# Adding expert rows per token tile on TensorE, in PSUM, in a two-layer mixture-of-experts step

## The chip, the cores and the metric

The kernel runs on one core of one Trainium2 chip. The metric is the device time of one execution, in microseconds (us). Lower is better.

## The reference, cut to what matters

A step of a two-layer transformer over 384 tokens (128 of context, 256 latent), model width 1024, everything in float32. Each layer mixes tokens (three kinds of attention and an output projection), and then applies a mixture of experts, which is what the change touches:

```python
def hier_moe(h, router_group, router_expert, w_gate, w_up, w_down):   # 4 groups of 8 experts, FF = 256
    g_sel = argmax(ht @ router_group)                  # one group per token
    top_v, top_i = lax.top_k(e_in, 2)                  # two experts inside it
    top_w = softmax(top_v) * g_w                       # their two weights
    y = sum over the two experts e of  top_w_e * (silu(ht @ w_gate[e]) * (ht @ w_up[e])) @ w_down[e]
x = layer_norm(ALPHA * x + gate * y, ln2_w, ln2_b)     # ALPHA = 4 ** 0.25, ends the layer
```

Each of the 384 tokens sends one row to each of two of 32 experts. Each expert has 3 MB of weights (three matrices of 1 MB), so a layer reads 96 MB of expert weights.

## The kernel before, in words

The five engines have one instruction stream each and meet through semaphores. `x` holds the tokens in three tiles of 128 (tile 0 context). A layer is: a front (projections, attention, output projection, first layer norm, router), the expert loop, possibly an item loop, and the end (weighting, second layer norm).

**Experts.** The 32 experts are worked in 16 pairs. A pair has 128 slots, 64 for each expert (`SLOTS`). From the ranks of tokens inside their experts, VectorE builds one-hot marks and TensorE turns them into indices (`select`, `places_of`, `indices`). GpSimd fetches the 128 token rows of a pair by an indirect DMA from `token_rows` in HBM (`fetch`, L2225), TensorE turns them (`rows_T`, L1215) and multiplies (`hidden`, L1243: the two experts stand in the two column halves of the array, products with 64 stationary columns; `down`, L1267). ScalarE and VectorE copy one half each of the 128 result rows of width 1024 (`rows_half`, L1555 and L2046) into one of two buffers `yb`, and GpSimd writes them by an indirect DMA to `expert_rows` in HBM (`scatter`, L2231), at row 1 + 2 * token + choice.

**Items.** Rows of rank 64 and above of an expert don't fit. `most` and `overflow` on VectorE find the pairs that have such rows, and write a list. An item (`item` on each engine) is one pair and one further round of 64 slots per expert. Its marks and indices are made ahead, for the first item in the expert loop at pairs 10 and 11 (`ITEM_STEP`), its six weight blocks are loaded by SyncE (`load_item`, L844), its matmuls are L1215, L1276, L1324, L1332 and L1344, and its rows go to `expert_rows` by L2247. The loop count is read from memory on every engine.

**End of a layer.** When all scatters have landed, ScalarE issues three reads (L1640), one per tile: each token's two rows, 1 MB. VectorE then takes, tile by tile, first row times first weight (L2172), plus second row times second weight (L2173), times `gate2` (L2174), plus ALPHA * x (L2176), moments (L1854, L1860, L1861), and the normalisation (`normalise`, L1869, then L1871 with a power that GpSimd makes, L2218). `ln2_done` counts the tiles; TensorE turns a tile for the next layer's front (L957) when its count has come, and goes on with the projections (L969, L962).

**Order of loads.** SyncE issues all weight loads in program order, each 1 MB into one of 17 places (12 in `ring`); each waits for the unit that lay there. `places_of_loads` works the places out ahead. In the last 12 freed ring places of a layer come the item's weights, `ln2` and `gate2`, and the first loads of the next layer. Expert weights are prefetched as far as places come free.

Of the kernel before, what the change touches and what calls it, by code (L numbers as in the profile page):

```python
# [21 lines left out]
U32 = mybir.dt.uint32  # L22
ALU = mybir.AluOpType
# [3 lines left out]
P = 128  # L27
# [32 lines left out]
ROUNDS_MAX = TOKENS // SLOTS  # L60
# [4 lines left out]
OVER_CODES = (ROUNDS_MAX - 1) * PAIRS  # L65
# [51 lines left out]
GATH = (7168, 9216, 3072)  # L117
# [4 lines left out]
K_COS = K_IOTA + SLOTS  # L122
# [11 lines left out]
K_MHALF = K_THR + ROUNDS_MAX  # L134
K_TOK = K_MHALF + 3
K_CODE = K_TOK + TILES
K_16 = K_CODE + OVER_CODES
K_COLS = K_16 + ROUNDS_MAX - 2


def shape_constants():
# [8 lines left out]
    k[:, K_IOTA:K_IOTA + SLOTS] = np.arange(SLOTS)  # L150
# [24 lines left out]
    k[:, K_THR:K_THR + ROUNDS_MAX] = SLOTS * np.arange(ROUNDS_MAX)  # L175
# [4 lines left out]
    k[:, K_16:K_16 + ROUNDS_MAX - 2] = PAIRS * np.arange(1, ROUNDS_MAX - 1)  # L180
# [121 lines left out]
LATE = ("ln2", "gate2")  # L302
# [35 lines left out]
def places_of_loads():  # L338


    spots, items, late, last_in, count = {}, [], [], [], [0] * PLACES
    free = deque((p, None) for p in range(RING))
    for l in range(DEPTH):
# [10 lines left out]
        items.append(left[:PAIR_UNITS])  # L354
        late.append(dict(zip(LATE, left[PAIR_UNITS:])))
        last_in.append({spots[l, u][0]: (l, u) for u in gone})
        free = deque(left[PAIR_UNITS + len(LATE):] + [(p, (l, ("item", m))) for m, (p, _) in enumerate(items[l])]
                     + [(late[l][n][0], (l, ("late", n))) for n in LATE])
    return spots, items, late, last_in


SPOT, ITEM_SPOT, LATE_SPOT, LAST_IN = places_of_loads()


# [3 lines left out]
ITEM_STEP = PAIRS - 5  # L368

# [35 lines left out]
def build(nc, x_prompt, x_sample, c, cache_na_k, cache_na_v, state_ret, cache_diff_k, cache_diff_v, c_ctx,  # L405
# [12 lines left out]
    with ExitStack() as ctx:  # L418
# [94 lines left out]
        osel = at(GSEL, TILES, 2, SLOTS)  # L513
# [4 lines left out]
        gath = [at(i, 2, D) for i in GATH]  # L518
# [8 lines left out]
        tab = route(TILES, PAIRS, 4)  # L527
        idxf = route(PAIRS * 2)
        idxu = route(PAIRS * 2).bitcast(U32)
        oidxf = route(2)  # L530
        oidxu = route(2).bitcast(U32)
        orow = route(1).bitcast(U32)
# [10 lines left out]
        pmax = route(PAIRS)  # L543
# [4 lines left out]
        steps = route(ITEMS_MAX, ROUNDS_MAX - 2)  # L548
        shift = route(ITEMS_MAX)
        n_items = route(1)  # L550
        iotar = route(SLOTS)
# [17 lines left out]
        rows_out = [signal(f"rows_out{i}", 16 * PAIRS // 2) for i in range(2)]  # L569
# [58 lines left out]
        o_full = [signal(f"o_full{s}", 16) for s in range(PAIR_UNITS)]  # L628
# [8 lines left out]
        o_out, o_stored = signal("o_out", 16), signal("o_stored", 1, start=1)  # L637
# [26 lines left out]
        def item_pair(eng, l, rel):  # L664

            return eng.value_load(items[0:1, bass.ds(l * ITEMS_MAX + rel, 1)], min_val=0, max_val=PAIRS - 1)
# [9 lines left out]
        def wait_released(eng, l, unit):  # L676
# [22 lines left out]
            elif kind == "late":  # L699
                eng.wait_ge(ln2_done.sem, ln2_done.at(l, TILES))  # L700
            elif kind == "pair":
# [23 lines left out]
        def _(sp):  # L725
# [29 lines left out]
            def late_loads(l):  # L755

                for name in LATE:
                    wait_released(sp, *LATE_SPOT[l][name][1])
                    for k in range(2):
                        if name == "ln2":  # L760
                            sp.dma_start(late_tile(l, name, k), (ln2_w, ln2_b)[k][l:l + 1].to_broadcast([P, D]))\
                                .then_inc(ln2_in.sem, 16)
                        else:
                            sp.dma_start(late_tile(l, name, k), modd[l, 1, k:k + 1, D:2 * D].to_broadcast([P, D]))\
                                .then_inc(gate2_in.sem, 16)
# [69 lines left out]
            def load_item(l, o0, i):  # L835

                p = item_pair(sp, l, item_place(l, o0, i))
                for m in range(PAIR_UNITS):
                    kind, which = m // 2, m % 2
                    place, (_, (_, pair, part, _)) = ITEM_SPOT[l][m]  # L840
# [3 lines left out]
                    sp.dma_start(ring[:, place, :], expert_unit(l, 2 * p + which, kind)).then_inc(o_full[m].sem, 16)  # L844

            sp.wait_ge(cond_zero.sem, 3)
            for l in range(DEPTH):
# [6 lines left out]
                if l:  # L854
                    for t in range(TILES):
                        sp.wait_ge(gathered[t].sem, gathered[t].at(l - 1, 16))
# [26 lines left out]
                late_loads(l)  # L883
# [9 lines left out]
        def _(pe):  # L893
# [296 lines left out]
            def first_places(l, tiles):  # L1190

                for j in tiles:
                    pe.wait_ge(pair0_marked.sem, pair0_marked.at(l, j + 1))
                    mm = pe.matmul(ps[:, IDX_BANK[0], 0:4], gsel[:, j, 0:2, :].rearrange("p e s -> p (e s)"),
                                   tab[:, j, 0, :], start=(j == 0), stop=(j == TILES - 1))
# [3 lines left out]
            def places_of(l, k):  # L1199
# [5 lines left out]
                for i in range(a, b):  # L1205
                    e = 2 * (i % GPAIRS)
                    for j in range(TILES):
                        mm = pe.matmul(ps[:, IDX_BANK[k], 2 * e:2 * e + 4],  # L1208
                                       gsel[:, j, e:e + 2, :].rearrange("p e s -> p (e s)"),
                                       tab[:, j, i, :], start=(j == 0), stop=(j == TILES - 1))  # L1210
# [62 lines left out]
            def item_index(p):  # L1273

                for j in range(TILES):
                    mm = pe.matmul(ps[:, 7, 0:4], osel[:, j, :, :].rearrange("p e s -> p (e s)"),  # L1276
                                   tab[:, j, bass.ds(p, 1), :].rearrange("p o k -> p (o k)"),
                                   start=(j == 0), stop=(j == TILES - 1))
                mm.then_inc(o_idx.sem, 1)

            def experts(l):
# [6 lines left out]
                for i in range(PAIRS):  # L1288
# [10 lines left out]
                    if i == ITEM_STEP:  # L1299
                        first = items_before(pe, l)  # L1300
                        p = item_pair(pe, l, 0)
                        pe.wait_ge(o_sel.sem, o_sel.at(first + l, 1))
                        pe.wait_ge(xt_dve.sem, xt_dve.at(l, i + 2))
                        item_index(p)
                    hidden_T(l, i)

            def item(l, o0, i):

                pe.wait_ge(o_xr_in.sem, o_xr_in.at(i, 16 * (l + 1)))
# [4 lines left out]
                p = item_pair(pe, l, item_place(l, o0, i, 1))  # L1314
                pe.wait_ge(o_xt_dve.sem, o_xt_dve.at(i, 1))
                pe.wait_ge(o_sel.sem, o_sel.at(i + l, 2))
                item_index(p)
# [1035 lines left out]
```

## Time and profile before

| | |
|---|---|
| timed runs | 1209.1, 1213.51, 1214.12 us (median 1213.51) |
| profiled execution | span 1211.0 us (the page has no other time of it), 16524 instructions |
| PE (TensorE) busy | 1053.2 us, 87% |
| PE weight loads | 703.2 us, 58% |
| DVE (VectorE) | 432.5 us, 36% |
| ACT (ScalarE) | 209.3 us, 17% |
| POOL (GpSimd) | 181.7 us, 15% |
| DMA | 343.83 MB in 102993 packets, mean 284 GB/s |

The profile is of one execution. Engines overlap, so busy shares say little about what sets the end; that is read from the chain of waits, which is followed back from the last instruction. In 40 slices of the span TensorE and the DMA engines look like this (digits are tenths, GB/s is what the DMA engines moved):

```profile
PE   4899999989979999987739999999896999998840
...
PEclk9799999999879999989859999999995999999985
DMA  8997222685999999999869312238957899999961
```

Layer 0 ends in slices 20 and 21 (from 577 to 623 us), layer 1 in the last two. The long stretches of 9 in the DMA line are the expert loops.

### The profile page before, as it was taken

How to read it: one execution, taken by the hardware profiler on the slowest of the kernel's cores; microseconds unless marked ns; L12 is line 12 of the kernel's file. 1: busy time of each engine (PE TensorE's matmuls, PEld its weight loads, DVE VectorE, ACT ScalarE, POOL GpSimd, SP SyncE). 2: the span in 40 equal slices, each digit the busy share in tenths (PEclk: the TensorE clock that was granted, in tenths of full speed). 3: DMA queues.
4: the chain of work that ended last, by engine and by line, in shares of the span. 5: the costliest groups of instructions: out<-in, count | busy, mean ns of one | idle time of the engine just before them, and what ended most of it. 6: DMA issues, size and time to landing. Idle time of an engine off the chain costs nothing.

```text
span 1211.0 us, 16524 instructions
## 1 busy us (share of the span) xinstructions
PE 1053.2 (87%) x6588; PEld 703.2 (58%) x6589; DVE 432.5 (36%) x1016; ACT 209.3 (17%) x524; POOL 181.7 (15%) x176
## 2 busy tenths in 40 slices
PE   4899999989979999987739999999896999998840
PEld 1766878568655555554328577775785655554510
DVE  0044544257741212100164344543676212111117
ACT  0322334100111111101113222421001111111000
POOL 0440020051111111101113000202301111111001
PEclk9799999999879999989859999999995999999985
DMA  8997222685999999999869312238957899999961
GB/s 345 251 276 230 70 83 71 229 293 236 352 420 417 419 419 418 418 420 419 317 225 319 99 64 77 83 110 314 332 182 286 349 418 419 418 419 419 410 247 63
DMA packets 102993, 343.83 MB, mean 284 GB/s; under 512 B 20530, under 2 KB 61538, under 8 KB 70404
## 3 DMA queue, kind: packets, MB, share of 16 engines
q1 hardware_dynamic: 88832, 316.58, 68.6%
q0 software_dynamic: 12352, 16.74, 4.5%
q10 hardware_dynamic: 1732, 9.45, 2.0%
q8 instruction: 54, 0.88, 0.3%
q14 instruction: 23, 0.19, 0.0%
HBM read 341.92 MB, written 26.16 MB: 304 GB/s over the span
## 4 chain that ended last, share of the span: by engine, by line
PE 63%; SPq 13%; DMA 11%; DVE 4%; issue 4%; POOL 3%; ACT 2%; POOLq 0%; DVEq 0%; ACTq 0%
PE ps L969 16%; SPq L828 13%; PE ps L1243 11%; PE ps L962 8%; PE ps L1146 7%; PE ps L1267 5%; DMA arena<-in_exp_w_gate 2%; DMA ring<-in_exp_w_down 2%; DMA arena<-in_exp_w_down 2%; PE ps L1215 2%; DMA ring<-in_w_mod 2%; PE ps L911 1%; PE ps L1062 1%; PE ps L1208 1%; PE ps L1108 1%
## 5 line engine op out<-in xcount | busy, mean ns | idle before, releaser
L1243 PE MATMUL ps<-ring,arena 128*64 128x256 f32 x1488 | 208.7, 402 | 14.4 <-DMA ring<-in_exp_w_up 6.8
L969 PE MATMUL ps<-ring,arena 128*128 128x256 f32 (+1 forms) x960 | 200.8, 367 | 5.8 <-ACT arena L1477 5.8
L969 PEld LDWEIGHTS ps<-ring,arena 128*128 128x128 f32 x960 | 170.9, 195 | 28.9 <-issue 8.6
L1243 PEld LDWEIGHTS ps<-ring,arena 128*64 128x64 f32 x1488 | 128.4, 144 | 70.1 <-issue 27.7
L1267 PE MATMUL ps<-ring,arena 128*64 128x512 f32 x360 | 96.6, 608 | 10.0 <-DMA ring<-in_exp_w_down 7.5
L2039 DVE TENSOR_TENSOR arena<-arena,ps 128x256 f32<-128x256 f32 x32 | 13.5, 421 | 253.8 <-PE ps L1243 143.3
L962 PE MATMUL ps<-arena,ring 128*128 128x384 f32 x288 | 96.9, 490 | 0.7 <-ACT arena L1482 0.5
L1146 PE MATMUL ps<-ring,arena 128*128 128x256 f32 x384 | 90.0, 398 | 0.0
L1146 PEld LDWEIGHTS ps<-ring,arena 128*128 128x128 f32 x384 | 76.8, 202 | 11.4
L2225 POOL DMA_INDIRECT arena<-token_rows,arena x32 | 33.4, 1045 | 279.1 <-PE ps L1215 154.0
L962 PEld LDWEIGHTS ps<-arena,ring 128*128 128x128 f32 x288 | 53.3, 190 | 36.8 <-issue 1.8
L1555 ACT ACTIVATE arena<-ps 128x512 f32<-128x512 f32 x32 | 19.1, 597 | 255.3 <-PE ps L1267 255.3
L2046 DVE COPY arena<-ps 128x512 f32<-128x512 f32 x32 | 22.1, 692 | 108.5 <-PE ps L1267 108.5
L1267 PEld LDWEIGHTS ps<-ring,arena 128*64 128x64 f32 x360 | 28.8, 138 | 51.2 <-issue 48.7
L2231 POOL DMA_INDIRECT expert_rows<-arena x32 | 33.0, 1031 | 159.2 <-DVE arena L2046 157.3
L1215 PE MATMUL ps<-kc,arena 128*128 128x128 f32 x264 | 48.6, 308 | 7.3 <-DMA arena<-token_rows,arena 4.3
L911 PE MATMUL ps<-ring,cond 128*32 128x512 f32 x360 | 48.9, 653 | 6.6 <-DMA ring<-in_w_mod 6.6
L1215 PEld LDWEIGHTS ps<-kc,arena 128*128 128x128 f32 x264 | 35.2, 196 | 32.4 <-issue 25.0
L1243 PE MATMUL ps<-arena 128*64 128x256 f32 x320 | 49.4, 395 | 3.1 <-DMA arena<-in_exp_w_up 2.3
L1482 ACT ACTIVATE arena<-ps 128x256 f32<-128x256 f32 (+2 forms) x60 | 24.6, 415 | 152.2 <-PE ps L969 104.1
L2218 POOL TENSOR_TENSOR ln_s<-ln_s,kc 128x1 f32<-128x1 f32 x12 | 18.3, 1526 | 145.7 <-DVE ln_s L1861 145.7
L1243 PEld LDWEIGHTS ps<-arena 128*64 128x64 f32 x320 | 30.0, 141 | 13.3 <-issue 3.5
(264 smaller groups left out, 1279.1 us busy)
## 6 DMA issues: line engine op xcount, KB each, us to landing
ring<-in_exp_w_gate SPq DMA_DIRECT2D x49, 1024.0 KB, 21.3
ring<-in_exp_w_up SPq DMA_DIRECT2D x48, 1024.0 KB, 21.7
ring<-in_exp_w_down SPq DMA_DIRECT2D x47, 1024.0 KB, 28.5
ring<-in_w_mod SPq DMA_DIRECT2D x45, 1024.0 KB, 5.5
ring<-in_w_in SPq DMA_DIRECT2D x24, 1024.0 KB, 13.2
arena<-in_exp_w_down SPq DMA_DIRECT2D x12, 1024.0 KB, 20.1
arena<-in_exp_w_up SPq DMA_DIRECT2D x11, 1024.0 KB, 24.2
arena<-in_exp_w_gate SPq DMA_DIRECT2D x9, 1024.0 KB, 29.1
```

Of the source, the lines that this page charges most:

```text
L828: sp.dma_start(dst, src).then_inc(ring_full[place].sem, 16)
L911: mm = pe.matmul(ps[32 * g:32 * g + 32, bank, 0:512], cond[:, ch, :], weights[:, 512 * g:512 * g + 512], start=(ch == 0), stop=(ch == CH - 1))
L962: mm = pe.matmul(out[:, 0:TOKENS], w[:, ch, :], hT[:, ch, :], start=(ch == 0), stop=(ch == CH - 1))
L969: mm = pe.matmul(out[:, 0:w], hT[:, ch, where * P:(where + 1) * P], unit(l, name)[:, ch, 0:w], start=(ch == 0), stop=(ch == CH - 1))
L1146: mm = pe.matmul(ps[:, 2 * t + u // 2, (u % 2) * UCOL:(u % 2 + 1) * UCOL], mixed(ch, t), unit(l, name)[:, ch, :], start=(ch == 0), stop=(c ...
L1215: mm = pe.transpose(ps[:, 7, k * P:(k + 1) * P], src[:, 4 * b + k::CH], ident)
L1243: mm = pe.matmul(ps[64 * w:64 * w + 64, 2 * (i % 2) + kind, 0:FF], xgT[i % 2][:, ch, w * SLOTS:(w + 1) * SLOTS], weights[:, ch * FF:(ch + ...
L1267: mm = pe.matmul(ps[64 * w:64 * w + 64, 5 + n, :], hidT[i % 2][:, j, 64 * w:64 * w + 64], weights[:, j * D + n * 512:j * D + (n + 1) * 512 ...
L1482: act.activation(dst, job_view(j, n, dst), ACT.Copy, scale=RET_SCALE if kind == "rkT" else 1.0)\
L2046: dve.tensor_copy(yb[i % 2][:, 512:D], ps[:, 6, :]).then_inc(row_dve.sem, 1)
L2225: pool.indirect_dma_start(xr[i % 2], None, h2d, bass.IndirectOffsetOnAxis(ap=idxu[:, 2 * i + 1:2 * i + 2], axis=0), bounds_check=TOKENS, o ...
L2231: pool.indirect_dma_start(rows, bass.IndirectOffsetOnAxis(ap=idxu[:, 2 * i:2 * i + 1], axis=0), yb[i % 2], None, bounds_check=ROWS - 1, oo ...
```

## The change

1. **The last pair's rows** (pair 15) are no longer scattered (`SCATTERED = 15`). VectorE makes, for this pair, a matrix of marks times gate weights (`marks_of_last`, after `gate_weights`, at pair 11), TensorE turns it into `ptl` (at pair 12) and at the end multiplies it with `yb[1]`, per tile.
2. **Items** are one expert with 128 slots. Their marks times gate weight are turned into `pti[t]`; their rows stay in `yi`. Before an item overwrites them, the rows of the item before are flushed: six products into PSUM, and VectorE adds them times gate2 / ALPHA to x. The first item flushes zeros. An item loads three weight blocks and stores nothing.
3. **Weighting.** The two gathered rows of a token are multiplied by diagonal matrices of the two weights (zero for rows that were never scattered) in the same PSUM banks (`final_sums`). VectorE multiplies by gate2 from PSUM (`combine`) and goes on as before, in the order combine 0, 1, normalise 0, combine 2, normalise 1, 2.
4. **Reading back** is issued by SyncE into ring places, after `gate2` has been loaded ahead of the items, and before the next layer's first loads; tile 2's after `ln2`.
5. `expert_rows` is set to zero once, in layer 0, by eight DMAs of GpSimd from the `decay` tile.

```diff
+ITEM_SLOTS = 2 * SLOTS
+SCATTERED = PAIRS - 1
+FINAL_BANKS = ((4, 7), (0, 1), (2, 3))
+FLUSH_BANKS = ((2, 3), (5, 6), (4, 2))
...
 # SyncE, end of a layer
+                load_gate2(l)
                 wait_alone(sp, items_known, items_known.at(l, 1))
...
-                late_loads(l)
+                for k in range(2):
+                    wait_alone(sp, rows_out[k], rows_out[k].at(l, rows_out[k].step))
+                load_rows_back(l, 0)
+                load_rows_back(l, 1)
+                load_ln2(l)
+                load_rows_back(l, 2)
...
 # TensorE
+            def turn_marks(outs):
+                for j in range(TILES):
+                    mm = pe.transpose(outs[j], gw[:, j, :], ident)
+                return mm
...
+            def final_sums(l, o1):
+                pe.wait_ge(row_act.sem, row_act.at(l, PAIRS))
+                pe.wait_ge(row_dve.sem, row_dve.at(l, PAIRS))
+                pe.wait_ge(pt_copied.sem, pt_copied.at(l, 1))
+                pe.wait_ge(pi_zeroed.sem, pi_zeroed.at(l, 1))
...
+                for t in range(TILES):
+                    outs = [ps[:, FINAL_BANKS[t][n], :] for n in range(2)]
+                    halves_ = [slice(512 * n, 512 * n + 512) for n in range(2)]
+                    for n in range(2):
+                        pe.matmul(outs[n], ptl[:, t, :], yb[(PAIRS - 1) % 2][:, halves_[n]], start=True, stop=False)
+                    for n in range(2):
+                        pe.matmul(outs[n], pti[t], yi[:, halves_[n]], start=False, stop=False)
+                    pe.wait_ge(gathered[t].sem, gathered[t].at(l, 16))
+                    for k in range(2):
+                        for n in range(2):
+                            mm = pe.matmul(outs[n], diag(k, t), gath(l, t)[:, k, halves_[n]], start=False, stop=(k == 1))
+                    mm.then_inc(final_ready.sem, 1)
...
+            def flush_half(t, n):
+                return pe.matmul(ps[:, FLUSH_BANKS[t][n], :], pti[t], yi[:, 512 * n:512 * n + 512], start=True, stop=True)
             def item(l, o0, i):
...
+                pe.wait_ge(pi_zeroed.sem, pi_zeroed.at(l, 1))
+                pe.wait_ge(row_act.sem, row_act.at(l, PAIRS))
+                pe.wait_ge(row_dve.sem, row_dve.at(l, PAIRS))
+                for t in range(TILES - 1):
+                    for n in range(2):
+                        mm = flush_half(t, n)
+                    mm.then_inc(o_flush.sem, 1)
+                flush_half(TILES - 1, 0)
                 pe.wait_ge(o_xr_in.sem, o_xr_in.at(i, 16 * (l + 1)))
...
                 for kind, done in ((0, o_gate), (1, o_up)):
...
                     for ch in range(CH):
-                        for w in range(2):
-                            mm = pe.matmul(ps[64 * w:64 * w + 64, kind, 0:FF],
-                                           xgT[0][:, ch, w * SLOTS:(w + 1) * SLOTS],
...
+                        mm = pe.matmul(ps[:, kind, 0:FF], xgT[0][:, ch, :],
+                                       ring[:, ITEM_SPOT[l][kind][0], ch * FF:(ch + 1) * FF],
...
+                    if kind == 0:
+                        pe.wait_ge(o_flushed.sem, o_flushed.at(i, 1))
+                        flush_half(TILES - 1, 1).then_inc(o_flush.sem, 1)
+                pe.wait_ge(o_gw.sem, o_gw.at(i, 1))
+                turn_marks([ps[:, 3, t * P:(t + 1) * P] for t in range(TILES)]).then_inc(o_pt.sem, 1)
...
 # ScalarE, in an item
+                act.wait_ge(o_pt.sem, o_pt.at(i, 1))
+                for t in range(TILES):
+                    ins = act.activation(pti[t], ps[:, 3, t * P:(t + 1) * P], ACT.Copy)
+                ins.then_inc(o_pi.sem, 1)
...
 # VectorE, in an item
+                for t in range(TILES):
+                    dve.wait_ge(o_flush.sem, o_flush.at(i, t + 1))
...
+                    for n in range(2):
+                        ins = dve.scalar_tensor_tensor(zt[:, half], ps[:, FLUSH_BANKS[t][n], :], 1.0 / ALPHA, gate2[:, half], ALU.mult, ALU.mult)
...
+                    dve.tensor_tensor(x[:, t, :], x[:, t, :], zt, ALU.add).then_inc(o_flushed.sem, 1)
...
 # VectorE, after the expert loop
+                for t in range(TILES):
+                    for k in range(2):
+                        ins = dve.tensor_scalar(diag(k, t), ident, wtsm[:, k, t:t + 1], None, ALU.mult)
+                ins.then_inc(diag_ready.sem, 1)
...
                 rows_half(l, PAIRS - 1)
+                dve.wait_ge(rows_out[0].sem, rows_out[0].at(l, rows_out[0].step))
+                dve.wait_ge(hidT_ready.sem, hidT_ready.at(l, PAIRS))
+                for t in range(TILES):
+                    ins = dve.memset(pti[t], 0.0)
+                ins.then_inc(pi_zeroed.sem, 1)
+                dve.wait_ge(gate2_in.sem, gate2_in.at(l, gate2_in.step))
...
+                combine(l, 0, chain)
+                combine(l, 1, chain)
+                normalise(l, 0, chain)
+                combine(l, 2, chain)
+                normalise(l, 1, chain)
+                normalise(l, 2, chain)
...
 # GpSimd
+                if l == 0:
+                    for n in range(ZERO_STEPS):
+                        pool.dma_start(rows[1 + n * 96:1 + (n + 1) * 96]..., zeros).then_inc(rows_zeroed.sem, 16)
...
-                    scatter(l, i)
+                    if i < SCATTERED:
+                        scatter(l, i)
```

`rows_out[0]` counts the scatters of the even pairs; its last one is now pair 14's. `yb[0]`, from which that scatter reads, is a scratch tile of the flush.

## Rows read from the trace of the kernel before

**Rows 1.** The page: the span, and the chain that ended last, by engine.

```profile
span 1211.0 us, 16524 instructions
...
PE 63%; SPq 13%; DMA 11%; DVE 4%; issue 4%; POOL 3%; ACT 2%; POOLq 0%; DVEq 0%; ACTq 0%
```

**Rows 2.** The chain of waits, 640 to 1160 us: start, duration (us), what.

```profile
649.29 13.83 PE ps L969 x64
...
1041.73 3.63 PE ps L1243 x32
...
1129.38 28.47 DMA ring<-in_exp_w_down
```

**Rows 3.** SyncE's waits, 700 to 840 us: total us, times, longest.

```profile
SPq L828 <- PE ps L969: 95.1, 7, 19.2
```

**Rows 4.** Timeline, end of layer 0: start, us, engine, line, operation [idle before].

```profile
577.91 0.97 POOL L2231 DMA_INDIRECT expert_rows<-arena  x1 [14.57 <-DVE arena L2046]
...
581.23 0.71 PE L1215 MATMUL ps<-kc,arena 128*128 128x128 f32 x4
...
581.34 0.69 DVE L2046 COPY arena<-ps 128x512 f32<-128x512 f32 x1 [4.28 <-PE ps L1267]
...
585.69 1.44 PE L1276 MATMUL ps<-arena 128*128 x6 [2.35 <-DVE arena L2055]
...
587.06 9.55 PE L1324 MATMUL ps<-ring,arena 128*64 128x256 f32 x64
...
598.18 3.65 PE L1344 MATMUL ps<-ring,arena 128*64 128x512 f32 x16 [0.47 <-ACT arena L1564]
...
601.88 0.69 DVE L2085 COPY arena<-ps 128x512 f32<-128x512 f32 x1 [4.74 <-PE ps L1344]
...
613.36 0.75 DVE L2172 TENSOR_SCALAR arena<-arena 128x1024 f32<-128x1024 f32 x1 [10.78 <-DMA arena<-expert_rows]
...
621.55 1.28 DVE L1871 SCALAR_TENSOR_TENSOR x<-x,ln_s,ring 128x1024 f32<-128x1024 f32 x1 [0.53 <-POOL ln_s L2218]
...
622.98 1.94 PE L957 MATMUL ps<-kc,x 128*128 128x128 f32 x8 [21.14 <-DVE x L1871]
...
627.15 10.01 PE L969 MATMUL ps<-ring,arena 128*128 128x256 f32 x32 [2.23 <-ACT arena L1477]
```

**Rows 5.** Timeline, end of layer 1, same columns.

```profile
1168.01 0.69 DVE L2046 COPY arena<-ps 128x512 f32<-128x512 f32 x1 [3.94 <-PE ps L1267]
...
1177.37 0.75 DVE L2172 TENSOR_SCALAR arena<-arena 128x1024 f32<-128x1024 f32 x1 [8.66 <-DMA arena<-expert_rows]
...
1179.47 1.22 DVE L2174 TENSOR_TENSOR arena<-arena,ring 128x1024 f32<-128x1024 f32 x1
...
1183.74 1.28 DVE L1869 SCALAR_TENSOR_TENSOR x<-x,ln_s,ring 128x1024 f32<-128x1024 f32 x1
...
1204.26 1.28 DVE L1871 SCALAR_TENSOR_TENSOR x<-x,ln_s,ring 128x1024 f32<-128x1024 f32 x1 [0.51 <-POOL ln_s L2218]
```

**Rows 6.** Landing time of the scatter issued at 577.91 us (line 2231).

```profile
DMA to landing us min/median/max: 8.4/8.4/8.4
```

**Rows 7.** Landing time of the scatter issued at 1164.93 us (line 2231).

```profile
DMA to landing us min/median/max: 4.1/4.1/4.1
```

**Rows 8.** The chain of waits at the end of layer 1.

```profile
1172.57 4.77 DMA arena<-expert_rows
```

**Rows 9.** Windows: length, busy (x) PE/PEld/DVE/ACT/POOL, granted clock, DMA share, GB/s.

```profile
578.00:582.00 4.00, 3.94 (x20) 1.55 (x16) 0.66 (x1) 0.62 (x2) 0.88 (x1) 1.00 1.00 406
...
586.00:588.00 2.00, 2.00 (x12) 1.60 (x13) 0.74 (x4) 0.00 (x0) 0.00 (x0) 0.50 0.86 349
...
592.00:594.00 2.00, 2.00 (x22) 1.31 (x20) 0.00 (x0) 0.39 (x1) 0.00 (x0) 1.00 0.56 217
```

**Rows 10.** VectorE groups by line and shape: busy us, mean ns.

```profile
L1692 DVE TENSOR_SCALAR decay<-kc,lg 128x128 f32<-128x128 f32 x12 | 2.5, 280 | 0.0
...
L1733 DVE TENSOR_TENSOR arena<-arena,kdec 128x384 f32<-128x384 f32 x8 | 3.9, 554 | 10.5 <-PE ps L962 10.5
```

More of the change, by code:

```diff
@@ L338, in places_of_loads @@
 def places_of_loads():
-    spots, items, late, last_in, count = {}, [], [], [], [0] * PLACES
+    spots, items, late, gath, last_in, count = {}, [], [], [], [], [0] * PLACES
     free = deque((p, None) for p in range(RING))
@@ L568, in build @@
         xr_in = [signal(f"xr_in{i}", 16 * PAIRS // 2) for i in range(2)]
-        rows_out = [signal(f"rows_out{i}", 16 * PAIRS // 2) for i in range(2)]
+        rows_out = [signal(f"rows_out{i}", 16 * len(range(i, SCATTERED, 2))) for i in range(2)]
         y_out = signal("y_out")
@@ L835, in load_item @@
             def load_item(l, o0, i):
[L837 to L840, printed above, removed]
+                e = item_expert(sp, l, item_place(l, o0, i))
+                for kind in range(ITEM_UNITS):
+                    place, (_, (_, pair, part, _)) = ITEM_SPOT[l][kind]
                     last, before = (gate_ready, up_ready, down_ready)[part], (o_gate, o_up, o_down)[kind]
@@ L843, in load_item @@
                     sp.wait_ge(before.sem, before.at(i, 0))
-                    sp.dma_start(ring[:, place, :], expert_unit(l, 2 * p + which, kind)).then_inc(o_full[m].sem, 16)
+                    sp.dma_start(ring[:, place, :], expert_unit(l, e, kind)).then_inc(o_full[kind].sem, 16)
             sp.wait_ge(cond_zero.sem, 3)
@@ new lines, in combine @@
+            def combine(l, t, chain):
+                zt = gath(l, t)[:, 1, :]
+                b0, b1 = FINAL_BANKS[t]
+                dve.wait_ge(final_ready.sem, final_ready.at(l, t + 1))
+                dve.tensor_tensor(zt.rearrange("p (a b) -> p a b", a=2), ps[:, b0:b1 + 1:b1 - b0, :],
+                                  late_tile(l, "gate2", min(t, 1)).rearrange("p (a b) -> p a b", a=2), ALU.mult)                    .then_inc(combined.sem, 1)
+                dve.wait_ge(combined.sem, combined.at(l, t + 1))
+                chain.link(dve.scalar_tensor_tensor(x[:, t, :], x[:, t, :], ALPHA, zt, ALU.mult, ALU.add))
+                moments(t, chain, var2)
@@ L2065, in item_indices @@
-                ins.then_inc(o_link.sem, 1)
+                token = ps[:, 7, 0:1]
+                dve.tensor_scalar(oidxf, token, 0.5, kc[:, K_EMPTY:K_EMPTY + 1], ALU.is_lt, ALU.mult).then_inc(o_link.sem, 1)
                 dve.wait_ge(o_link.sem, o_link.at(nth * 2, 2))
-                for w in range(2):
-                    hp, src = halves(7, 0, 1, w)
-                    ins = dve.tensor_tensor(oidxu[hp, :], oidxf[hp, :], src, ALU.add)
-                ins.then_inc(o_known.sem, 1)
+                dve.tensor_tensor(oidxu, oidxf, token, ALU.add).then_inc(o_known.sem, 1)
@@ L2142, in _ @@
                 copy_rows_T(l, 0)
-                most(l, chain)
                 overflow(l, chain)
```

304 lines of the change are left out of this document (170 added, 134 removed).

## The prediction

> **What bounds the kernel now.** I read the chain of waits first. Of the 1211.0 us span TensorE holds 63%, SyncE's queue 13%, DMA 11% [rows 1]. In layer 1 the chain runs on TensorE's own projections until pair 7's products at 1041.7 us, then on the weight stream (SyncE's queue), whose last block was issued at 1129.4 and landed 28.5 us later [rows 2]: up to there the layer is set by TensorE, after it by the stream. While TensorE sets it, SyncE waits for it (95.1 us for line 969 alone, [rows 3]), so nothing in the front of layer 1 is ahead of TensorE, and a late start of layer 1 moves everything behind it one for one. The weight stream does not absorb it: its ring places are freed by that same TensorE.
>
> So the change is worth what it does in two stretches, the two layer ends, read from the timeline. Layer 0: the last pair's rows are copied out by 582.03; one overflow item runs from 581.23 to 602.57 (21.3 us); its store and the reading back take until 613.36; tile 0 is finished at 622.83, and only then does TensorE turn it for layer 1 (622.98) [rows 4]. Layer 1 has no item: rows copied out by 1168.70, first weighted row at 1177.37, last normalisation ending 1205.54, then 5.5 us to the end [rows 5].
>
> **The number of items** depends on the data. The reference's router gives, on the kernel's inputs, one expert with 65 tokens in layer 0 (number 28; its neighbour has 40) and none above 64 in layer 1. So both kernels run one item in layer 0. It fetches three weight blocks in place of six, but its matmuls start without a wait for them now (index product ends 587.13, line 1324 starts 587.06 [rows 4]): the 3 MB saved are worth nothing.
>
> **The price of the new products.** 64 instructions of line 969 are 32 products of a 128x128 block with 256 columns and take 13.83 us [rows 2], 0.43 us each. With 512 columns that is 0.86; I take 0.87. The expert matmuls work on two column halves side by side and cost the same per pair, so a half-empty item gains nothing by being one expert: gate and up are 16 products of 256 columns, 6.9 us. The final sums are, per tile, 2 (last pair) + 2 (item) + 4 (two gathered rows times diagonal weights) products of 512 columns: 8 x 0.87 = 7.0 us, for three tiles 20.9 us, where TensorE had nothing to do. VectorE loses two steps per tile: its first tile was at 1177.37 to 1179.47 before the gate2 product, 2.1 us. What is left is a combine of 4.3 us (1179.47 to 1183.74) and a normalisation of 2.6 (two of 1.28) [rows 5]: 6.9 per tile. So TensorE and VectorE now pace each other at 7 us a tile.
>
> **Layer 1's end.** The memsets of the item's marks wait for the scatter of pair 14, issued 1164.93, landed 4.1 us later [rows 7]: 1169.03. Three memsets of 128x128 have no row; below, nothing, above, 0.28 us each (a tensor_scalar of that shape [rows 10]); I take 0.6 in all. TensorE starts at 1169.7, does four products (3.5) to 1173.2. SyncE issues the first read-back behind the same landing, at 1169.2; it took 4.77 [rows 8]: 1174.0. Tile 0's sum is ready at 1174.0 + 3.5 = 1177.5, tile 1's at 1184.5, tile 2's at 1191.4. VectorE: combine tile 2 to 1195.7, normalise tile 1 to 1198.3, tile 2 to 1200.9, against 1205.54: -4.6. For a lowered clock (below) I give back 0.5: **-4.1 us**. Pair 15's scatter (landing 1172.4) is what this end no longer waits for.
>
> **Layer 0's end.** Here the same memsets cost more. Pair 14's scatter was issued at 577.91 and took 8.4 us [rows 4, 6], because the weight queue was full (406 GB/s in that window [rows 9]): 586.3, plus 0.1 and 0.6, 587.0. The item in TensorE waits for it; its first instruction was at 581.23 [rows 4], so 5.8 us of a new wait. Behind it on TensorE is all of the item. (The queue is shorter now by 3 MB of item weights and the late rows, but still holds some 4 MB, about 10 us at 406 GB/s; so I keep 8.4, with the 4.1 of [rows 7] as the other end.)
> - Flush: five products, 4.35 us, though nothing has been summed yet for a first item. TensorE will have idled 5.7 us. In this trace it idled from 583.3 to 585.7 and then ran at clock 0.50 until about 592 (1.2 instead of 2.4 GHz) [rows 4, 9]; about 5.4 us at half speed lose 2.7. So 594.1.
> - Turning rows and making marks: 581.23 to 585.69 before [rows 4], and on VectorE one more product of 128x384 (0.55 [rows 10]) and a register load, less the three small mark instructions joined in one: +0.2, 598.8. Index product 1.4: 600.2.
> - Gate and up 6.9, the sixth flush product 0.9, and the same clock loss as now: line 1324 took 9.55 for 2 x 3.63 at full clock [rows 2, 4], 2.3. 610.2. VectorE's three flushed tiles (two 128x512 products and an addition of 128x1024, 2.7 each) end at 609.5, beside it.
> - Mark transposes 0.6, transposes of the hidden rows 0.5, ScalarE's three mark copies ahead of its hidden copy (1.1 + 0.4), four down products 3.5, copy 0.7: 616.6, against 602.57.
> - Final sums: 623.6, 630.6, 637.5. The reading back is done long before. VectorE takes combine 0, combine 1 and only then normalises tile 0: 630.6 + 4.3 + 2.6 = 637.5, against 622.83: +14.7.
> - The front of layer 1 then starts with a TensorE that was just busy. Before, its first 32 instructions of line 969 took 10.0 us [rows 4] for 6.9 by [rows 2]; ScalarE's drain of the turned tile, nearly 3 us, lies between, so I count back 1.0 only: **+13.7 us**.
>
> **What is hidden.** The gate weights, marks and diagonals (some 20 small VectorE instructions a layer, 0.3 to 0.6 us each, about 7 us) and the last pair's transposes stand in the expert loop, where the weight stream sets the time; without that cover they would cost up to 7 us a layer. The eight zeroing DMAs (3.1 MB, 8 us at 406 GB/s) are issued on GpSimd near 93 us of layer 0, ahead of its diff normalisation, long before VectorE needs them; uncovered, +8. SyncE's read-backs stand before layer 1's first weight loads; these are then issued near 590, needed after 637. The small loads, now behind these, come earlier than now.
>
> One rule speaks against the change. VectorE's six diagonals (0.28 us each [rows 10]) now run from about 577.1 to 578.8, beside the scatter issued at 577.91 [rows 4]. The Trainium skill (SBUF — State Buffer, "SBUF: two separate sides") says that a DMA issued by GpSimd cannot write its descriptors while VectorE runs an operation that takes both of its port pairs. By it the scatter, and with it the memsets, would be up to 0.9 us later in each layer, and the sum about 1.8 higher; no run here shows that yet.
>
> **Sum.** +13.7 - 4.1 = +9.6: the profiled span of 1211.0 becomes 1220.6. The page gives no other time for that execution; the timed runs' median is 1213.5 (1209.1 to 1214.1), 2.5 above the span. So 1223.
>
> **Rivals.**
> - *The item starts without the wait and with a fast clock.* If the scatter of pair 14 lands in 4.1 us or sooner and TensorE keeps its clock through the flush, layer 0 loses 4.3 + 2.7 less: +6.7, total +2.6, 1216. For it: the queue is shorter. Against: the six scatters issued between 545 and 584 us took 8.2 to 8.6, and [rows 6] is one of them.
> - *Not slower: the loss of layer 0 is absorbed.* If the weight stream of layer 1, which sets the time from 1041.7 on, could start as early as before, only the front would be late and the end would keep its -4.1: 1209.4. It decides from the point where SyncE is not waiting for TensorE. Against: [rows 3]; I give it little. The same result would come if the sums' products overlapped more than those of line 969.
> - *The cold clock reaches the final sums.* If TensorE's 1.5 us idle in layer 1 and the 1 us in the item let it fall, each end loses another 2.7: +15, 1228.5.
> - *The change does not do what it says:* more items than one. Each further one would add about 27 us (587.0 to 616.6, less the cold clock's 2.7); the router's counts speak against it.
>
> **Chances.** Forecast 0.58; first rival 0.15; absorbed 0.10; cold clock 0.13; rest 0.04. A difference of 0.5% (6 us) is about what can be told here: faster is below 1207.4 and gets 0.08 (half of the absorbed case, whose 1209.4 carries a few us of its own, and most of the rest); same, up to 1219.6, gets 0.22 (the first rival, the other half of the second, the lowest of the forecast's own spread); slower 0.70. The range 1211 to 1231 leaves out half of the absorbed case and the far tail.
>
> **What would show it.** Right: a TensorE gap of about 5 us before the item; line 957 of layer 1 near 637; sums of 7 us a tile, VectorE waiting for them; last normalisation 4 us earlier after the last copy than now. Wrong: the item's first product before 584, sums under 5 us a tile, or a weight stream in layer 1 that ends less than 10 us later than before.

## The result, and the profile after

| | before | after |
|---|---|---|
| timed runs | 1210.51 us median of 10 (1208.83 to 1215.79) | 1216.86 us median of 10 (1213.75 to 1220.08) |
| profiled execution | span 1211.0 us | span 1218.2 us, its own time 1220.08 us |

The ratio is 1.0049 with a 95% interval of 1.0033 to 1.0064: the changed kernel is 6 us slower. The prediction's 1223 us stands on the three runs of before that were known then (median 1213.5); all ten have their median 3.0 us lower. A profile is one execution, and executions of one kernel differ by some us: that of the changed kernel is the slowest of its ten (3.2 us above their median). So differences of whole spans are rough, and the readings below go by stretches and by the timed runs. In the sections below, line numbers are those of the kernel that the row is from.

The page of the changed kernel: the span, TensorE's and VectorE's busy time, the chain by engine [rows 1].

```profile
span 1218.2 us, 16695 instructions
...
PE 1099.9 (90%) x6665; PEld 724.6 (59%) x6666; DVE 437.7 (36%) x1042; ACT 210.8 (17%) x531; POOL 181.6 (15%) x181
...
PE 64%; SPq 13%; DMA 10%; DVE 5%; issue 4%; ACT 2%; POOL 2%; DVEq 0%; POOLq 0%; ACTq 0%
```

TensorE is busy 46.7 us longer, VectorE 5.2 us. Where that meets the path to the end is seen in the timeline. First the end of layer 0 (start, us, engine, line, operation, idle before it and what ended that), which answers to [rows 4]:

```profile
577.85 0.97 POOL L2363 DMA_INDIRECT expert_rows<-arena  x1 [14.85 <-issue]
...
580.92 0.69 DVE L2127 COPY arena<-ps 128x512 f32<-128x512 f32 x1 [3.07 <-PE ps L1304]
586.11 0.45 DVE L2299 MEMSET arena<- 128x128 f32 x3 [4.50 <-DMA expert_rows<-arena]
...
586.77 7.00 PE L1385 MATMUL ps<-arena 128*128 128x512 f32 x10 [5.88 <-DVE arena L2299]
...
593.60 0.60 PE L1252 MATMUL ps<-kc,arena 128*128 128x128 f32 x4
...
598.63 1.43 PE L1313 MATMUL ps<-arena 128*128 x6 [3.03 <-DVE arena L2173]
...
616.09 0.69 DVE L2211 COPY arena<-ps 128x512 f32<-128x512 f32 x1 [4.93 <-PE ps L1433]
617.09 1.96 PE L1347 MATMUL ps<-arena 128*128 128x512 f32 x4 [1.04 <-ACT arena L1662]
...
624.23 1.23 DVE L2161 TENSOR_TENSOR ring<-ps,ring 128x1024 f32<-128x1024 f32 x1 [7.45 <-PE ps L1353]
...
631.10 1.23 DVE L2161 TENSOR_TENSOR ring<-ps,ring 128x1024 f32<-128x1024 f32 x1 [2.52 <-PE ps L1353]
...
636.67 1.28 DVE L1959 SCALAR_TENSOR_TENSOR x<-x,ln_s,ring 128x1024 f32<-128x1024 f32 x1
...
638.11 1.13 PE L994 MATMUL ps<-kc,x 128*128 128x128 f32 x8 [0.18 <-DVE x L1959]
...
641.88 8.83 PE L1006 MATMUL ps<-ring,arena 128*128 128x256 f32 x32 [2.64 <-ACT arena L1563]
```

The reader is to see three things. The memsets of the item's marks wait for a scatter that was issued at 577.85, and TensorE stands idle for 5.88 us behind them. Then come 7.00 us of flush (line 1385) before the item's first row is turned (line 1252, 593.60). And the three sums end at 637.93, when VectorE has just finished tile 0 (637.95): the two engines arrive together, so another order on VectorE alone could start layer 1 no more than 0.2 us earlier. From the last pair's copy (580.92) to the turning of tile 0 for layer 1 (line 994) it is 57.19 us, against 41.64 before (581.34 to 622.98).

The end of layer 1 answers to [rows 5]:

```profile
1182.09 0.69 DVE L2127 COPY arena<-ps 128x512 f32<-128x512 f32 x1 [2.76 <-PE ps L1304]
...
1184.06 1.95 PE L1347 MATMUL ps<-arena 128*128 128x512 f32 x4 [2.02 <-DVE arena L2299]
...
1187.57 3.67 PE L1353 MATMUL ps<-ring,arena 128*128 128x512 f32 x8
...
1191.28 1.23 DVE L2161 TENSOR_TENSOR ring<-ps,ring 128x1024 f32<-128x1024 f32 x1 [8.08 <-PE ps L1353]
...
1198.14 1.23 DVE L2161 TENSOR_TENSOR ring<-ps,ring 128x1024 f32<-128x1024 f32 x1 [2.51 <-PE ps L1353]
...
1213.11 1.28 DVE L1959 SCALAR_TENSOR_TENSOR x<-x,ln_s,ring 128x1024 f32<-128x1024 f32 x1
```

From the copy to the last normalisation it is 31.02 us, against 36.25: 5.2 us are gained. The sums come every 6.87 us, and VectorE waits for TensorE (2.5 us before the second). From there on it waits no more: the third sum is ready when VectorE is free for it (1205.0). The rest is in the last few us, where SyncE waits for the other engines once its stores have landed. SyncE's waits, of before and then of after:

```profile
SPq L418 <- PEq L418: 2.6, 1, 2.6
```

```profile
SPq L428 <- PEq L428: 1.0, 1, 1.0
```

From the end of the last normalisation to the end of the span it is 5.5 us before and 3.8 after; 1.6 of that 1.7 us is this wait for TensorE's queue.

So the account of the profile is: end of layer 0 +15.6, its last copy 0.4 earlier, the stretch from line 994 to layer 1's last copy -1.1 (543.98 against 545.03 us), end of layer 1 -5.2, tail -1.7; together +7.2, which is the difference of the spans. The 0.4 and the 1.1 us are small against what this middle stretch does from one execution to another (540.9 to 544.1 us in the nine kernels with the change).

### The profile page after: what moved, and what is told of

Its sections match the earlier page's. It is cut to its first block, busy times and chain, and to the rows that moved or that the text cites. A ratio compares the mean times of both kernels' runs of the same rounds, so it can differ in the third digit from the quotient of the medians.

```text
span 1218.2 us, 16695 instructions
## 1 busy us (share of the span) xinstructions
PE 1099.9 (90%) x6665; PEld 724.6 (59%) x6666; DVE 437.7 (36%) x1042; ACT 210.8 (17%) x531; POOL 181.6 (15%) x181
## 4 chain that ended last, share of the span: by engine, by line
PE 64%; SPq 13%; DMA 10%; DVE 5%; issue 4%; ACT 2%; POOL 2%; DVEq 0%; POOLq 0%; ACTq 0%
PE ps L1006 16%; SPq L863 13%; PE ps L1280 10%; PE ps L999 7%; PE ps L1183 7%; PE ps L1304 5%; DMA ring<-in_exp_w_down 2%; DMA ring<-in_exp_w_gate 2%; DMA arena<-in_exp_w_down 2%; PE ps L1252 2%; DMA ring<-in_w_mod 2%; PE ps L948 1%; PE ps L1099 1%; PE ps L1245 1%; PE ps L1353 1%
## 5 line engine op out<-in xcount | busy, mean ns | idle before, releaser
L1280 PE MATMUL ps<-ring,arena 128*64 128x256 f32 x1488 | 205.1, 398 | 15.2 <-DMA ring<-in_exp_w_up 7.4
L1304 PE MATMUL ps<-ring,arena 128*64 128x512 f32 x360 | 96.5, 607 | 12.8 <-DMA ring<-in_exp_w_down 10.4
L1614 ACT ACTIVATE arena<-ps 128x384 f32<-128x384 f32 (+3 forms) x42 | 22.1, 527 | 89.0 <-PE ps L1119 60.8
## 6 DMA issues: line engine op xcount, KB each, us to landing
ring<-in_w_in SPq DMA_DIRECT2D x24, 1024.0 KB, 12.8
```

Source lines behind the costliest of these rows:

```text
L1280: mm = pe.matmul(ps[64 * w:64 * w + 64, 2 * (i % 2) + kind, 0:FF], xgT[i % 2][:, ch, w * SLOTS:(w + 1) * SLOTS], weights[:, ch * FF:(ch + ...
L1304: mm = pe.matmul(ps[64 * w:64 * w + 64, 5 + n, :], hidT[i % 2][:, j, 64 * w:64 * w + 64], weights[:, j * D + n * 512:j * D + (n + 1) * 512 ...
L1614: act.activation(dst, src, ACT.Copy).then_inc(probsT_copied.sem, 1)
```

## The experiments

Each kernel is timed beside the kernel before on its own chip. The table goes by the profile, with the two stretches just read, "layer 0" (start of the last copy to the turning of tile 0) and "layer 1" (start of the last copy to the start of the last normalisation step), in us:

| kernel | layer 0 | layer 1 | span | timed median, ratio to before (95%) |
|---|---|---|---|---|
| before | 41.64 | 36.25 | 1211.0 | 1210.51 |
| after | 57.19 | 31.02 | 1218.2 | 1216.86, 1.0049 (1.0033 to 1.0064) |
| e1_late_wait | 49.81 | 31.11 | 1209.6 | 1209.04, 0.9992 (0.9974 to 1.0009) |
| e2_no_flush | 49.44 | 31.00 | 1209.3 | 1210.67, 1.0002 (0.9985 to 1.0019) |
| e3_no_flush_no_wait | 42.38 | 30.99 | 1204.3 | 1202.28, 0.9933 (0.991 to 0.9956) |
| e6_flush_if_needed | 43.15 | 31.10 | 1203.6 | 1205.4, 0.9955 (0.9935 to 0.9975) |
| e8_products_if_needed | 43.51 | 29.34 | 1203.0 | 1203.41, 0.9938 (0.9919 to 0.9957) |
| e4_before_no_items | 23.95 | 36.27 | 1194.1 | 1192.63, 0.9838 (0.9811 to 0.9865) |
| e5_after_no_items | 23.75 | 31.04 | 1181.3 | 1185.45, 0.9795 (0.9761 to 0.983) |
| e7_no_item_products | 53.30 | 29.15 | 1211.1 | 1214.25, 1.0021 (1.0003 to 1.0039) |
| e9_last_pair_scattered | 53.39 | 35.89 | 1218.2 | 1220.74, 1.008 (1.0052 to 1.0109) |

### The wait for the scatter (e1)

VectorE waits for the scatter only ahead of the flush of x (and once more ahead of the combines), no longer ahead of the memsets that TensorE waits for.

```diff
-                dve.wait_ge(rows_out[0].sem, rows_out[0].at(l, rows_out[0].step))
                 dve.wait_ge(hidT_ready.sem, hidT_ready.at(l, PAIRS))
                 ...
+                dve.wait_ge(rows_out[0].sem, rows_out[0].at(l, rows_out[0].step))
                 zt = yb[0]
```

> The changed kernel, but VectorE waits for pair 14's scatter only where it first needs the buffer (before the flush of the item), no longer ahead of the memsets that TensorE's item waits for. Theory (the new wait of 5 us stands on the path and also cools TensorE's clock): TensorE's gap before the item goes from 5.9 to about 1.5 us, the flush takes 4.3 us in place of 7.0, the whole is 7 us faster than the changed kernel (about 1211, no difference from before). Rival (the item is paced by VectorE's chain, and TensorE would wait for it later): less than 2 us faster, about 1216.

Measured: 1209.04 us, ratio 0.9992, as the theory of the wait had it; layer 0 is shorter by 7.4 us. The timeline of e1 at the item's start:

```profile
581.58 0.45 DVE L2299 MEMSET arena<- 128x128 f32 x3
...
582.23 4.53 PE L1385 MATMUL ps<-arena 128*128 128x512 f32 x10 [1.36 <-DVE arena L2299]
...
586.60 0.60 PE L1252 MATMUL ps<-kc,arena 128*128 128x128 f32 x4
```

The idle time falls from 5.88 to 1.36 us, and the same five products take 4.53 instead of 7.00 us. The clock in windows shows why (length, busy time of PE/PEld/DVE/ACT/POOL, granted clock, DMA share, GB/s), first of after, then of e1:

```profile
587.00:590.00 3.00, 3.00 (x4) 1.25 (x5) 0.00 (x0) 0.00 (x0) 0.00 (x0) 0.50 0.89 314
590.00:592.00 2.00, 2.00 (x4) 0.79 (x3) 0.00 (x0) 0.00 (x0) 0.00 (x0) 0.57 1.00 406
592.00:594.00 2.00, 2.00 (x9) 1.04 (x7) 0.00 (x0) 0.00 (x0) 0.00 (x0) 1.00 0.99 408
```

```profile
582.00:584.00 2.00, 1.77 (x4) 0.87 (x5) 0.03 (x1) 0.00 (x0) 0.00 (x0) 1.00 0.41 170
584.00:586.00 2.00, 2.00 (x6) 0.95 (x5) 0.00 (x0) 0.00 (x0) 0.00 (x0) 1.00 0.30 125
```

After the long gap TensorE runs at 1.2 GHz, after the short one at 2.4. So the wait costs 4.5 us of idle time and 2.5 us of clock, 7.0 of the 7.4.

### The flush (e2, e3)

e2 takes the six flush products and VectorE's part of them out; e3 also lets the item start without the wait, which then stands only where `yi` and `pti` are written. With one item in layer 0 and none in layer 1, the flush adds zeros.

```diff
-                for t in range(TILES - 1):
-                    for n in range(2):
-                        mm = flush_half(t, n)
-                    mm.then_inc(o_flush.sem, 1)
-                flush_half(TILES - 1, 0)
...
-                    if kind == 0:
-                        pe.wait_ge(o_flushed.sem, o_flushed.at(i, 1))
-                        flush_half(TILES - 1, 1).then_inc(o_flush.sem, 1)
```

> The changed kernel without the flush of the item's rows (six products on TensorE, nine instructions on VectorE), which adds nothing where a layer has one item; the wait for pair 14's scatter stays where it is. Theory (the flush is on the path in full): 7.0 us for the first five products, 1 for the sixth, less about 0.5 for transposes that now run at the low clock: 7.5 us faster than the changed kernel, about 1210. Rival (flush hidden beside the rows' turning and VectorE's marks): under 2 us.

> Both: no flush, and the item on TensorE starts as soon as its rows are there, as in the kernel before. Theory: 5.4 us of wait, 7.0 and 1.0 of flush, 13.4 us faster than the changed kernel, about 1203.5, that is 0.5 to 0.6% faster than before. Rival (the front of layer 1 or the weight stream absorbs part): half of that, about 1210.

Measured: e2 1210.67 us, 1.0002, and e3 1202.28 us, 0.9933. Set against the changed kernel by the ratios that is 5.7 us less (expected 7.5) and 14.0 less (expected 13.4); layer 0 is 7.75 us shorter without the flush, 14.8 without both. In e2 the gap stays, and the transposes behind it pay the clock in place of the flush (1.09 us, where e3 takes 0.71):

```profile
586.19 1.09 PE L1252 MATMUL ps<-kc,arena 128*128 128x128 f32 x4 [6.39 <-DVE arena L2276]
```

```profile
581.51 0.71 PE L1252 MATMUL ps<-kc,arena 128*128 128x128 f32 x4
```

So the two costs add (wait 7.1 to 7.4, flush 7.4 to 7.75, together 14.8), and without them the end of layer 0 is within 0.7 us of before (42.38 against 41.64): from the item's rows to the turning of tile 0 the new sums take 21.8 us in e3, storing and reading back the item's rows and the weighting took 21.1 before.

### Both kernels without items (e4, e5)

```diff
-                chain.link(dve.tensor_scalar(later, found, 0.5, None, ALU.is_gt))
+                chain.link(dve.tensor_scalar(later, found, 1.0e9, None, ALU.is_gt))
```

e4 is the kernel before with this line and the eight zeroing DMAs, e5 the one after with this line.

> The kernel before with the item loop never entered (it leaves out the one row of rank 64 of layer 0) and with the eight zeroing DMAs of the change. It also shows what the zeroing costs. Theory (zeroing hidden): the item took 581.3 to 603.4; without it pair 15's scatter lands near 591 and the reading back ends near 596 in place of 613.4: 17 us faster than before, about 1193.5. Rival (the zeroing is on the path): 8 us less of a gain, about 1201.

> The changed kernel with the item loop never entered (the same row is left out). Theory (the change gains at a layer end without an item and loses by its item): the sums start near 587 in place of 617, 29 us faster than the changed kernel, about 1188, and about 5 us (2 to 7) faster than the kernel before without items. Rival (the weighting on TensorE is what makes the change slow, whatever the item does): slower than the kernel before without items, by 5 us or more.

Measured: 1192.63 against 1185.45 us. The ends of layer 0 are alike (23.95 and 23.75), the end of layer 1 is 5.2 us shorter, and the wait of the tail goes from 3.1 to 0.9 us; these two make 7.4 us, the medians differ by 7.2. The spans differ by 12.8 us; the 5.4 us more lie ahead of and between the ends. The profile of e4 is the slowest of its four runs (3.3 us above their median), that of e5 the fastest (2.3 below), which is as much, so they are left as spread between executions. Two things follow. Without items the change makes the kernel 7 us faster by the medians, 5 by the ratios (four runs each; the intervals of the ratios just overlap). And e4 came out as expected with the zeroing in it, so the 8 us of the zeroing are hidden. One trace of it is left: pair 14's scatter in layer 0 is issued 1.87 us after the start of its copy in e4, 1.86 in after and 1.54 in before, 0.3 us later with the zeroing; why is not shown.

### The item's products in the sums (e7), the last pair's rows (e9)

```diff
-                    for n in range(2):
-                        pe.matmul(outs[n], pti[t], yi[:, halves_[n]], start=False, stop=False)
```

> The changed kernel without the two item products of each tile's sum (it leaves out the item's rows; in layer 1 they add zeros). Six products a tile take 5.2 us, VectorE 6.9. Theory (TensorE sets the pace of both ends): layer 0's tile 0 is finished 4.3 us earlier (1.7 for the first sum, 2.6 because VectorE no longer waits for the second), layer 1 ends 2.4 us earlier, together 6.7 faster, about 1210. Rival (VectorE sets the pace already): under 1.5 us.

Measured: layer 0 3.9 us shorter, layer 1 1.9, together 5.8 for the 6.7 expected; timed 1214.25, by the ratios only 3.4 us better than after, half of what was expected, and this is not explained. (The spans differ by 7.1, but after's profile is its slowest run and this one lies 1.3 us under its median.) Four of the removed products stood ahead of the second sum, behind which VectorE finishes tile 0 (3.4 us), which is the price in layer 0. In layer 1 only the second tile's two products came off (1.7 us). The first sum now waits for the data, and from the second sum on VectorE sets the pace, so the third tile's are worth nothing:

```profile
1182.19 3.70 PE L1351 MATMUL ps<-ring,arena 128*128 128x512 f32 x8 [1.47 <-DMA ring<-expert_rows]
```

e9 scatters pair 15 again and drops the `ptl` products; the rest of the change stays.

```diff
-SCATTERED = PAIRS - 1
+SCATTERED = PAIRS
...
-                        pe.matmul(outs[n], ptl[:, t, :], yb[(PAIRS - 1) % 2][:, halves_[n]], start=True, stop=False)
```

> The changed kernel with the last pair scattered and read back as all others, so that six products a tile are left (item and gathered rows). Theory: layer 0 gains 4.3 us (as by leaving out the item's products; the later scatter has time to land), layer 1's reading back waits for pair 15's scatter, 4 us later, and gains 2.4 by the shorter sums: together 2.9 faster than the changed kernel, about 1213.5. Rival (keeping the last pair off HBM is what speeds up the end): slower by 4 us or more.

This expectation failed, and the rival's price was nearly met: timed 1220.74 us, by the ratios 3.8 us slower than after. (The spans are equal because this profile is its fastest run and after's its slowest.) Layer 0 is 3.8 us shorter, but layer 1 is 4.9 longer; that makes only 1.1 of the 3.8 us, the rest is not accounted for. Its timeline and its clock at the end of layer 1:

```profile
1178.62 0.97 POOL L2360 DMA_INDIRECT expert_rows<-arena  x1 [3.64 <-DVE arena L2125]
...
1182.56 0.80 SPq L798 DMA_DIRECT2D ring<-expert_rows  x2
...
1187.40 5.50 PE L1351 MATMUL ps<-ring,arena 128*128 128x512 f32 x8 [6.30 <-DMA ring<-expert_rows]
```

```profile
1184.00:1187.00 3.00, 0.00 (x0) 0.00 (x0) 0.00 (x0) 0.00 (x0) 0.00 (x0) 0.54 0.98 388
```

The read-back waits for one more scatter, TensorE idles 6.30 us, its clock falls to 0.54, and the first four products on the gathered rows take 5.50 us instead of 3.67. So keeping the last pair's rows out of the round trip is what earns the 5 us at the end of layer 1; it costs 3.8 us in layer 0, where the item hides that round trip.

### A version that beats both (e6, e8)

In e6 the flush runs only from a layer's second item on, behind branches on TensorE and VectorE, and TensorE's and VectorE's waits stand where e3 has them. Nothing is left out.

```diff
+                with pe.If(i > o0):
                     pe.wait_ge(pi_zeroed.sem, pi_zeroed.at(l, 1))
                     ...
                     flush_half(TILES - 1, 0)
+                with pe.If(i <= o0):
+                    pe.sem_inc(o_flush.sem, TILES)
```

> A complete version: as e3, but the flush stands in a branch that is taken from a layer's second item on. Theory: e3 plus a few branches on TensorE and VectorE, some 0.5 to 1.5 us: about 1204.5, 0.4 to 0.5% faster than before. Rival: a branch inside the loop costs more than 5 us on TensorE, and the gain over before is gone.

Measured: 1205.4 us, 0.9955, as expected. Layer 0 takes 43.15 us, 0.8 more than e3, which is the most that the branches can have cost there; 0.3 of it lies in the gate and up products (9.21 against 8.93 us). The timed medians lie 3.1 us apart, with intervals that overlap, so the whole price is not settled.

e8 adds `with pe.If(o1 > o0):` around the item's products in the sums.

> This is the version with the flush only from a layer's second item on (1205.4 us, ratio 0.9955, span 1203.6), and with the six products of the item's rows in the final sums issued only where the layer has an item at all. Theory: layer 0 has one item, so nothing changes there beyond three branches of TensorE; layer 1 has none and drops six products, 2.6 us of TensorE in all. Where these products were left out of both layers, layer 1's first sum then waited for the read-back of the scattered rows, so at most 1.8 us come off (the second and third tile), and the branches take some back: 1203.5 us, ratio 0.994. Rival: a branch on TensorE's queue inside each tile costs about 1 us (it can't run ahead of it), six of them in the two layers, and the version is slower than the one it is made from: 1207 us or more, ratio 0.998.

Measured: 1203.41 us, 0.9938, which is the theory's number. Layer 1 is 1.76 us shorter than in e6 and layer 0 0.4 longer, all of it in the gate and up products (9.57 against 9.21 us), ahead of the new branches; the rival's 1 us per branch is refuted. The 1.76 us are the second tile's products alone, as in e7, not the second and third tile's as expected. The timed gain of e8 over e6 (2.0 us, intervals that overlap) isn't settled by itself; the gain of either over before is.

## Why the prediction was right or wrong

**Layer 0's end: right, step by step.** Forecast for a last copy at 581.34; the measured starts are 0.42 us earlier for that reason alone.

| step | forecast | measured |
|---|---|---|
| item may start | 587.0 | 586.77 |
| flush done | 594.1 | 593.60 |
| marks ready | 598.8 | 598.63 |
| gate and up | 600.2 | 599.92 |
| item copied out | 616.6 | 616.78 |
| tile 0 finished | 637.5 | 637.95 |

Counted from the last copy that is +15.5 for +14.7. Half of the difference is arithmetic: the item's terms, as the prediction lists them from 610.2 on, add up to 617.0 and not 616.6. The warm clock at the front gave back 1.2 for 1.0 (line 1006: 8.83 us for its first 32, [rows 4] has 10.01). e1 and e3 give the two terms their sizes by removal. The wait with its clock is 7.4 us (forecast 5.8 + 2.7, less the 1.4 us by which the memsets hold TensorE in e1 too: 7.1). The flush is 7.4 us, the 1.4 us of the memsets with it, which e3 takes away as well (forecast 4.35 + 0.9 + 1.4: 6.7). Together 14.8 for 13.8.

**Why the scatter landed late: shown in part, and not as put.** The prediction kept 8.4 us "because the weight queue was full". It landed in 8.2, and in 3.2 in layer 1; but the DMA engines were only 0.57 to 0.69 busy at the issue, and 0.33 to 0.37 in the last 4 us of the wait, falling:

```profile
578.00:580.00 2.00, 2.00 (x12) 0.86 (x10) 0.00 (x0) 0.00 (x0) 0.82 (x1) 1.00 0.69 287
580.00:582.00 2.00, 0.88 (x5) 0.00 (x0) 0.69 (x1) 0.60 (x1) 0.00 (x0) 1.00 0.61 252
582.00:584.00 2.00, 0.00 (x0) 0.00 (x0) 0.00 (x0) 0.00 (x0) 0.00 (x0) 1.00 0.37 156
584.00:586.00 2.00, 0.00 (x0) 0.00 (x0) 0.00 (x0) 0.00 (x0) 0.00 (x0) 0.73 0.33 135
```

In e5, without the item's loads, the share was 0.19 at the issue and the read-back that waits for the same scatter was issued 3.6 us after it. So the other transfers matter. The packets by queue, q1 the loads and q0 GpSimd's DMAs (packets, MB, share of 16 engines), first from 582 to 583 us, then for the scatter of layer 1 from 1180 to 1181, show how:

```profile
q1 hardware_dynamic: 12, 0.10, 23.2%
q0 software_dynamic: 20, 0.06, 14.3%
```

```profile
q0 software_dynamic: 57, 0.16, 42.6%
```

In layer 0 loads kept 23% of the engines' time busy from 582 to 586 us, by estimate 3.7 of 16 engines, and the scatter's packets moved beside them from 579 us until it landed at 586. In layer 1 there were no loads beside it, and its packets were through within 2 us. So the queues were not full; a few engines that still had loads to move fit the rows, but no row shows single engines. The value was right, its reason only in part. (Of the "six scatters" that the prediction sets against its first rival the trace has four in that stretch, at 547.5, 562.4, 577.9 and 582.9 us; they landed in 8.2 to 8.6 us.) The Trainium skill (DMA: Bandwidth & Descriptors, "Anatomy of one DMA — SWDGE (gpsimd) path") gives a DMA of GpSimd 2.0 us plus its bytes at 436 GB/s, by which 128 rows of 4 KB take an estimated 3.2 us; the landing in layer 1 agrees, the one in layer 0 doesn't.

**Layer 1's end and what follows it: right in kind, mis-sized, and this is the step that failed.** Forecast -4.1 to the end of the program, measured -6.9: -5.2 to the last normalisation and -1.7 in the tail. Three parts: the 0.5 us given back for a lowered clock wasn't due (2.0 us of idle time did not lower it, the granted clock was 1.00 from 1184 to 1191 us); the sums came every 6.87 us instead of 7.0; and, the largest part, the tail was taken as fixed ("then 5.5 us to the end"). It isn't, it was 3.8: the end of the program holds a wait of SyncE for TensorE's queue that no term of the sum had. It was 2.6 and 3.1 us in the two kernels with the old end, 0.9 to 1.1 in all nine with the new one. What in TensorE's queue makes it longer isn't shown.

**The sum.** 9.6 forecast, 7.2 in the profile: +0.4 from layer 0, -1.1 from layer 1's end, -1.7 from the tail. The sum gives 1213.5 + 9.6 = 1223.1. Of the 6.2 us between that and 1216.9, 2.4 are this, 0.8 is that the timed medians differ by 6.3, less than the spans, and 3.0, the largest piece, are no cost of the change at all: they are the median of three runs, which was taken as the base without an allowance, though the three ran from 1209.1 to 1214.1. The direction was not luck: e1 to e3 confirm the mechanism behind it.

**The diagonals beside the scatter.** In layer 1 they ran while the scatter was being issued for 0.3 us:

```profile
1178.07 1.26 DVE L2291 TENSOR_SCALAR arena<-kc,arena 128x128 f32<-128x128 f32 x6
1179.01 0.98 POOL L2363 DMA_INDIRECT expert_rows<-arena  x1 [16.68 <-DVE arena L2127]
```

The issue took 0.98 us, as the others do (0.97 to 1.01), began 1.55 us after the start of its copy, as before (1.55), and landed in 3.2. In layer 0 the diagonals were done (577.86) when the issue began (577.85). That looks as if the scatter had waited for them, and it came 0.3 us later after its copy than before; but e4, which has the zeroing and no diagonals, has the same delay. The 0.9 us a layer that the rule of the Trainium skill (SBUF — State Buffer, "SBUF: two separate sides") would have cost did not appear; with so short an overlap that is no test of the rule.

**The rivals.** The first (fast landing, warm clock) was priced at 7.0 us off; e1, which makes it so, took 7.4 off. Absorption did not happen: TensorE turned tile 0 for layer 1 15.1 us later than before, and the last pair's copy at the other end of layer 1 was still 14.1 us later. The cold clock did not reach the final sums (gaps of 1.0 and 2.0 us ahead of them); e9 shows it does where the gap is 6.3 us. There was one item.

## What to carry to other kernels

Where a wait is moved ahead of a cheap instruction, ask which engine needs that instruction: here 0.45 us of memsets, needed by TensorE, stood behind a wait that only the flush of x needed, and cost 7 us. A path that prepares for a rare case (a second item) belongs behind a branch; in the profiles the branches cost under 1 us, the path 7 us. And count a round trip through HBM for each end by itself: taking it away earned 5 us where nothing hid it, and cost 4 where something did.

## What the runs showed of the hardware

- The granted clock: after 5.88 us without a product TensorE ran at 1.2 GHz for over 4 us (0.50 from 587 to 590, 0.57 to 592); after 1.36 and 2.0 us it stayed at 2.4. The 3.03 us gap ahead of line 1313, in which VectorE makes the item's marks, was preceded by short transposes with 0.7 us of idle time between them, and the clock was low behind it (0.57 from 598 to 602 and 0.58 to 606 in after, 0.50 from 591.6 to 595 in e1, 0.50 from 585.3 to 588 in e6), so the first of the item's gate and up products run at half speed, for 5 to 7 us, as they did before [rows 9]. No experiment went at that.
- The same scatter of 128 rows of 4 KB landed in 8.2 us with the DMA engines 0.57 to 0.69 busy at its issue and loads on 23% of their time or more until it landed, in 3.2 with 0.08 to 0.24.
- A branch on TensorE inside the final sums is not to be seen in them: in layer 0 the third tile's products start 6.86 us after the second's in e6, which has none, and 6.87 after in e8.
- The program's end had a wait of SyncE for TensorE's queue of 2.6 and 3.1 us in the two kernels in which TensorE's last products ended 36 us before the last normalisation, and of 0.9 to 1.1 us in the nine in which they ended 8 to 10 us before it. That the one causes the other is not shown.
